# A two-layer decoder trunk: the first mixer's attention with its values stationary, two heads on the array's column halves, and probabilities scaled on GpSimd

## The reference, cut to what matters

```
# dilated: 4 slots; a slot joins three heads (window, dilation) = (128,1), (512,4), (2048,16)
s = q . k * scale, masked;  lse = logsumexp(s);  p = exp(s - lse);  out_g = p @ v
alpha = softmax over the three groups of lse;  o = sum_g alpha_g * out_g      # = one softmax over the three maps
# native sparse (NSA): 8 query heads, 2 key/value heads, three branches with a gate each
o = gate0 * softmax(q.k_cmp) @ v_cmp + gate1 * softmax(q.k_slc) @ v_slc + gate2 * softmax(q.k_win) @ v_win
out = concat(o_nsa, o_dil) @ w_out
```

## Time and profile before

| | before |
|---|---|
| median of 3 runs | 689.08 us (687.07 to 690.55) |
| the profiled execution: its time | 689.5 us |
| the profiled execution: its span | 687.5 us |
| PE busy | 668.7 us, 97% |
| DVE, ACT, POOL busy | 67%, 55%, 22% |
| chain that ended last | 92% PE |

### The profile page before, as it was taken

The page is one execution under the profiler, slowest core; times in us unless marked ns, Lnnn a source line. Parts: engine busy times, 40 slices in busy tenths (PEclk is TensorE's granted clock), DMA queues, the critical chain, the costliest instruction groups (busy, mean ns, idle before and its releaser), DMA issues.

```text
span 687.5 us, 10253 instructions
## 1 busy us (share of the span) xinstructions
PE 668.7 (97%) x3719; PEld 560.3 (82%) x3719; DVE 459.3 (67%) x620; ACT 380.4 (55%) x539; POOL 154.0 (22%) x117
## 2 busy tenths in 40 slices
PE   4999999999999999999999999999999999999996
PEld 3888887778788888888887999777788888888885
DVE  4596775577776878786547563576676878786532
ACT  5556435476476666767334634375475757676320
POOL 0021220000122434343001000372113343444000
PEclk9999999999999999999999999999999999999999
DMA  8957643001365353544752745301545353634601
GB/s 337 400 200 268 220 161 122 1 2 62 123 215 213 131 236 131 235 147 182 292 189 109 274 159 237 127 1 53 193 160 211 148 225 141 236 130 184 245 0 61
DMA packets 18651, 116.20 MB, mean 169 GB/s; under 512 B 2463, under 2 KB 3133, under 8 KB 5693
## 3 DMA queue, kind: packets, MB, share of 16 engines
q1 hardware_dynamic: 17325, 111.52, 43.3%
q10 hardware_dynamic: 1296, 4.26, 1.8%
HBM read 114.72 MB, written 1.05 MB: 168 GB/s over the span
## 4 chain that ended last, share of the span: by engine, by line
PE 92%; DVE 2%; ACT 2%; issue 2%; POOL 1%; DMA 1%; DVEq 0%; POOLq 0%
PE ps L1516 22%; PE ps L1155 13%; PE ps L1157 13%; PE ps L1156 13%; PE ps L1518 11%; PE ps L1197 5%; PE ps L1351 3%; PE ps L1277 1%; PE ps L1311 1%; PE ps L1150 1%; PE ps L1567 1%; PE ps L1437 1%; PE ps L1556 1%; PE ps L1287 1%; POOL rstd L1070 1%
## 5 line engine op out<-in xcount | busy, mean ns | idle before, releaser
L629 DVE TENSOR_TENSOR wlo<-raw,whi 128x2048 fp32r<-128x2048 f32 x99 | 226.0, 2311 | 69.6 <-ACT whi L333 69.5
L1516 PE MATMUL ps<-xpair,whi 128*128 128x512 f32 x640 | 226.4, 399 | 0.0
L333 ACT CAST whi<-raw 128x2048 fp32r<-128x2048 f32 x99 | 186.1, 1916 | 71.2 <-PE ps L1157 66.8
L1518 PE MATMUL ps<-xpair,wlo 128*128 128x256 f32 x640 | 179.8, 281 | 0.0
L1516 PEld LDWEIGHTS ps<-xpair,whi 128*128 128x128 f32 x640 | 120.3, 188 | 29.9
L1518 PEld LDWEIGHTS ps<-xpair,wlo 128*128 128x128 f32 x640 | 120.9, 189 | 0.0
L1110 POOL TENSOR_TENSOR hidf<-act_g,conv 128x512 f32<-128x512 f32 x22 | 74.6, 3392 | 83.9 <-ACT act_g L533 83.9
L1157 PE MATMUL ps<-whi,hid_lo 128*128 128x512 f32 x176 | 69.4, 395 | 0.0
L1156 PE MATMUL ps<-wlo,hid_hi 128*128 128x512 f32 x176 | 69.4, 394 | 0.0
L1155 PE MATMUL ps<-whi,hid_hi 128*128 128x512 f32 x176 | 69.4, 394 | 0.0
L1155 PE MATMUL ps<-whi,xpair 128*128 128x512 f32 x168 | 67.2, 400 | 0.2
(11 more groups left out here) (174 smaller groups left out, 987.5 us busy)
## 6 DMA issues: line engine op xcount, KB each, us to landing
raw<-in_weights SPq DMA_DIRECT2D x101, 1024.0 KB, 4.9
c_gpre<-in_gpre ACTq DMA_DIRECT2D x4, 512.0 KB, 4.7
raw<-in_weights SPq DMA_DIRECT2D x4, 512.0 KB, 8.5
c_gpost<-in_gpost ACTq DMA_DIRECT2D x4, 512.0 KB, 4.9
h<-in_x SPq DMA_DIRECT2D x2, 512.0 KB, 7.7
out<-h SPq DMA_DIRECT2D x4, 256.0 KB, 2.0
t<-in_masks SPq DMA_DIRECT2D x1, 512.0 KB, 14.1
c_rope<-in_rope SPq DMA_DIRECT2D x1, 256.0 KB, 14.0
```

The costliest lines, as they stand in the source:

```text
L333: act.copy(whi[:, slot, :], raw[:, slot, :]).then_inc(hi_done, 1)
L629: dve.tensor_tensor(wlo[:, slot, :], raw[:, slot, :], whi[:, slot, :].bitcast(F32), ALU.subtract).then_inc(lo_done, 1)
L1516: pe.matmul(ps[:, b0 + m, :], whi[:, slot, cols], xpair[:, kt].rearrange("p a c -> p (a c)"), start=kt == 0, stop=kt == KT - 1, skip_group ...
L1518: ins = pe.matmul(ps[:, b0 + m, 0:SEQ], wlo[:, slot, cols], xhi[:, kt, :], start=False, stop=kt == KT - 1, skip_group_check=True)
```

## The change

- **Values stationary.** `it_values` becomes `dil_values` and `nsa_values`. The 64 columns of values of a head are the stationary operand and 128 tokens of `probsT` move. The result comes out turned already, so `out_turn` and its copies' source change: `tile_hi` and `tile_lo` read the result bank.
- **Two heads on column halves.** The results of head e go to PSUM partitions 64e to 64e + 63, that is to one column half of the array, and the instructions of the two heads alternate.
- **Scaling.** A result whose tokens lie along the free axis can't be scaled per token, so the probabilities are: `it_coefs` on DVE (reciprocal, times gate) and then `it_scale` on GpSimd, in place in `probs`. `it_turn(n)` now waits for `it_scaled`. `it_output` and the separate results of the compressed branch go; that branch is one more matmul in `nsa_values`.
- **Order.** Dilated items come in pairs (slots 0 and 1, then 2 and 3), each pair with `t` = 1 first. `dil_qk` makes the scores of both with alternating rows, and waits for the exponentials of both items before. NSA items have `t` = 1 first too. `probs` and `probsT` have three buffers instead of two.

```diff
-        ITEMS = [("dil", j, t) for j in range(SLOTS) for t in range(TT)] + \
-                [("nsa", i, t) for i in range(NSA_PER) for t in range(TT)]
+        ITEMS = [("dil", 2 * pair + e, t) for pair in range(SLOTS // 2) for t in reversed(range(TT)) for e in range(2)] + \
+                [("nsa", i, t) for i in range(NSA_PER) for t in reversed(range(TT))]
...
@@ ACT
             for n in range(NI + 2):
                 if n < NI:
                     it_turned_out(n)
+                if n in TILE_OUT:
+                    tile_hi(TILE_OUT[n])
+                if n + 2 < NI:
+                    it_probs(n + 2)
                 if n == 0:
                     act.wait_ge(unit_used, EVEN_END["unit", 6])
                     act.copy(vbuf[:, :, 768:1280], ps[:, 6:8, :]).then_inc(in_free_act, 1)
-                if n - 2 in TURNS:
-                    it_hi(n - 2)
-                if n + 2 < NI:
-                    it_probs(n + 2)
...
@@ DVE
+            it_coefs(0)
+            it_coefs(1)
             compressed_probs()
             for n in range(NI + 2):
+                if n + 2 < NI:
+                    it_maxima(n + 2)
+                if 1 <= n and n + 1 < NI:
+                    it_coefs(n + 1)
                 if n < NI:
                     it_turned_out(n)
...
@@ POOL
+            def it_scale(n):
+                kind, _, t = ITEMS[n]
+                w, s, v = P * (t + 1), n % 3, n % 4
+                pool.wait_ge(it_coef, coefs_until(n))
+                if kind == "dil":
+                    pool.tensor_scalar(probs[:, s, 0:NG * w], probs[:, s, 0:NG * w], coef[:, v, 0:1], None,
+                                       ALU.mult).then_inc(it_scaled, 1)
+                    return
+                for m in range(4):
+                    ins = pool.tensor_scalar(probs[:, s, m * w:(m + 1) * w], probs[:, s, m * w:(m + 1) * w],
+                                             coef[:, v, 4 + m:5 + m], None, ALU.mult)
+                ins.then_inc(it_scaled, 1)
...
@@ PE
+            def dil_qk(n):
+                t = ITEMS[n][2]
+                w, tok = P * (t + 1), slice(t * P, (t + 1) * P)
                 if n >= 2:
-                    pe.wait_ge(it_exp, exps[n - 2])
+                    pe.wait_ge(it_exp, exps_until(n - 1))
+                for g in range(NG):
+                    for e in range(2):
+                        hd = g * SLOTS + ITEMS[n + e][1]
+                        rows = slice(HD * e, HD * e + HD)
+                        pe.matmul(psh[:, s_half(n + e) + g, 0:w], qkT[rows, TDQ + hd // 2, tok],
+                                  qkT[rows, TDK + hd // 2, 0:w], start=g != 1, stop=False, skip_group_check=True)
...
             def it_turn(n):
-                pe.wait_ge(it_exp, exps[n])
+                pe.wait_ge(it_scaled, n + 1)
...
+            def dil_values(n):
+                t = ITEMS[n][2]
+                o = tile_out(n, n + 1)
+                for m in range(NG):
                     for kt in range(t + 1):
                         k = m * (t + 1) + kt
-                        ins = pe.matmul(ps[:, bank, col:col + HD], probsT[:, s, k * P:(k + 1) * P],
-                                        vbuf[:, kt, v0:v0 + HD], start=k == 0, stop=k == maps * (t + 1) - 1,
-                                        skip_group_check=True)
+                        for e in range(2):
+                            v0 = V_DIL + (m * SLOTS + ITEMS[n + e][1]) * HD
+                            ins = pe.matmul(o[e * HD:(e + 1) * HD, :], vbuf[:, kt, v0:v0 + HD],
+                                            probsT[:, (n + e) % 3, k * P:(k + 1) * P], start=k == 0,
+                                            stop=k == NG * (t + 1) - 1, skip_group_check=True)
+                ins.then_inc(it_pv, 2)
...
+            it_turn(0)
+            dil_qk(2)
+            pe.wait_ge(in_free_act, EVEN_ACT)
+            it_turn(1)
+            for n in range(2, ND, 2):
+                if n + 2 < ND:
+                    dil_qk(n + 2)
+                else:
+                    nsa_qk(ND)
                 it_turn(n)
+                dil_values(n - 2)
+                if n + 2 == ND:
+                    nsa_qk(ND + 1)
+                it_turn(n + 1)
+                if n + 1 == PC_TURN:
+                    compressed_turn()
+            for n in range(ND, NI - 1):
+                if n + 2 < NI:
+                    nsa_qk(n + 2)
+                it_turn(n)
+                if n == ND:
+                    dil_values(ND - 2)
+                else:
+                    nsa_values(n - 1)
...
+            out_blocks("out0", 0, EVEN_KT, xhi, xlo, 0, 1, operand)
+            it_turn(NI - 1)
+            nsa_values(NI - 2)
+            out_blocks("out0", 0, EVEN_KT, xhi, xlo, 1, 3, operand)
+            nsa_values(NI - 1)
+            out_blocks("out0", 0, EVEN_KT, xhi, xlo, 3, 5, operand)
```

More of the change, by code:

```diff
@@ L282, in maps_of, with exps_until, coefs_until @@
             return NG if ITEMS[n][0] == "dil" else 4
+        def exps_until(n):
+            return sum(1 if kind == "dil" else 4 for kind, _, _ in ITEMS[:n + 1])
+        def coefs_until(n):
+            return sum(1 if kind == "dil" else 2 for kind, _, _ in ITEMS[:n + 1])
         block = ctx.enter_context(nc.Block())
@@ L870, in it_turned_out @@
                 dve.wait_ge(it_turned, n + 1)
[L871 to L878, removed]
+                if n >= 3:
+                    dve.wait_ge(it_pv, n - 2)
+                dve.tensor_copy(probsT[:, n % 3, BLK:k], ps[:, 5, 0:k - BLK]).then_inc(it_pT1, 1)
@@ L1095, in _ @@
                                        ALU.add).then_inc(staged, 1)
+            def it_scale(n):
[10 more added lines that the diff above has]
+                ins.then_inc(it_scaled, 1)
+            for n in range(NI):
+                it_scale(n)
             def junction(p):
@@ L1332, in it_values, with tile_out @@
-            def it_values(n):
-                kind, j, t = ITEMS[n]
-                s, bank = n % 2, 6 + n % 2
-                pe.wait_ge(it_pT0, n + 1)
-                if t:
-                    pe.wait_ge(it_pT1, wide_before(n) + 1)
-                if n >= 2:
-                    pe.wait_ge(it_o, outs[n - 2])
-                    if n - 2 in TURNS:
-                        pe.wait_ge(ot_lo, turns_before(n - 2) + 1)
-                maps = maps_of(n)
-                for m in range(maps):
-                    if kind == "dil":
-                        v0, col = V_DIL + (m * SLOTS + j) * HD, 0
-                    else:
-                        v0, col = (V_SLC, V_WIN)[m % 2] + (m // 2) * HD, m * HD
+            def tile_out(n, last):
+                tile, t = TILE_OF[n], ITEMS[n][2]
+                pe.wait_ge(it_pT0, last + 1)
+                if t:
+                    pe.wait_ge(it_pT1, wide_before(last + 1))
+                if t == TT - 1 and tile >= 2:
+                    pe.wait_ge(ot_lo, tile - 1)
+                return ps[:, 6 + tile % 2, t * P:(t + 1) * P]
@@ new lines, in dil_values, with nsa_values @@
+                ins.then_inc(it_pv, 2)
+            def nsa_values(n):
+                _, j, t = ITEMS[n]
+                o = tile_out(n, n)
+                pe.matmul(o, vc[:, 2 * j:2 * j + 2, :].rearrange("p m d -> p (m d)"), pcT[:, t, :], start=True, stop=False,
+                          skip_group_check=True)
+                for br in range(2):
+                    for kt in range(t + 1):
+                        for g in range(NSA_G):
+                            k, v0 = (2 * g + br) * (t + 1) + kt, (V_SLC, V_WIN)[br] + g * HD
+                            ins = pe.matmul(o[g * HD:(g + 1) * HD, :], vbuf[:, kt, v0:v0 + HD],
+                                            probsT[:, n % 3, k * P:(k + 1) * P], start=False,
+                                            stop=br == 1 and kt == t, skip_group_check=True)
+                ins.then_inc(it_pv, 1)
```

176 lines of the change are left out of this document (57 added, 119 removed).

## The result

The changed kernel takes 704.04 us (median of 4 runs, 703.19 to 704.91) beside 689.82 us of the kernel before on the same chip: a ratio of 1.0216 with a 95% interval of 1.0198 to 1.0233. The prediction of 683.2 us, faster, was wrong in sign, and the time lies outside its range. The profiled execution took 703.19 us.

What follows compares the result with a forecast made beforehand. PE was taken as the bound, busy 668.7 of 687.5 us. First output block 6.74 us earlier minus 0.8 back gives 5.9; 689.5 - 5.9 - 0.4 = 683.2 us, range 680.5 to 691.

Steps and rivals of the forecast that it cites:

- I take the casts, since the operation has one tensor input: Scaling on POOL priced like one-input casts: 0.83 us for 768 columns, 1.6 for four maps of a t = 1 NSA item.
- the two-input line: Rival on POOL's scaling: two-input price, 1.9 us for 768 columns, 2.9 for four maps; 690.2 us, no change; chance 0.15.
- The dearest rival: DVE holds POOL's scaling up: 2.2 us for 768 columns, 4.2 for four maps; 695.9 us, slower; chance 0.05.
- It decides for slower from some 3.6 us for the four maps on: Threshold in the rival of DVE holding POOL up: the kernel gets slower from some 3.6 us of scaling per four maps.
- The chain over two NSA items: NSA part: turn, copy, exponentials, coefficients, scaling and hand-overs take 5.6 us, so PE stays the bound by 0.2 us.
- the clock: TensorE's clock in the stage: read as full in the dilated and NSA parts; the sum had no term for it.
- the three waits of the dilated part: PE waits 2.3 us for the vbuf copy ahead of turn 1, then 1.3 each ahead of scores 4 and 6.
- the values of a dilated pair: Dilated part, values on PE: 1.48 us per pair with t = 1, 0.84 with t = 0.
- column halves run beside each other: Values on PE: two heads' instructions overlap; the rival that they don't gives 692 us, slower by 0.4%, chance 0.06.
- 5.8 us per NSA pair: NSA part: PE's own work for a pair of items takes 5.8 us against 6.45 before.
- 41.8 us from turn 0 to the first block: Turn 0 at 113.7 us, first block of the output projection at 155.5 instead of 162.24.
- the 0.8 given back in the projection: Output projection: turn 15, values 14 and values 15, 2.65 us, fall into it, giving 0.8 us back.

Runs made afterwards that it cites:

- e3: The changed kernel with unused bf16 matmuls filling PE's waits in the dilated part and ahead of turns 8, 10, 12 and 14: 697.32 us.
- e11: The changed kernel with GpSimd's scaling as one two-tensor multiplication per item, coefficients broadcast along the columns: 689.99 us.
- e2: The changed kernel with the same scalings on VectorE, directly behind the item's coefficients, instead of on GpSimd: 688.49 us.
- e6: e2 with unused bf16 matmuls (11, 10, 10) in PE's three waits of the dilated part: 685.81 us.
- e4: The changed kernel with the scaling left out, each turn waiting for the coefficients alone: 685.63 us.
- e8: e2 with the vbuf copy ahead of item 2's exponentials, dilated values ahead of the next scores, and output projection blocks 3 and 4 as before the change: 686.64 us.
- e9: e2 with the vbuf copy ahead of item 2's exponentials, compressed probabilities behind item 2's maxima, and projection blocks 3 and 4 as before the change: 682.73 us.
- e12: e11 with e9's orders and projection tail, and exponentials 3 and 5 ahead of the copies of turns 1 and 3 on ScalarE: 683.0 us.

## Why the prediction was wrong

**The step that failed** is "I take the casts, since the operation has one tensor input". A float32 `tensor_scalar` on GpSimd does not run at the price of a cast: 2.26 us for 768 columns against 0.83, 3.69 for four maps against 1.6. The rows of before had a second reading, the two-input line, which I gave 0.15, and even that was too low (1.9 and 2.9). The dearest rival named nearly the right size, 2.2 and 4.2 us, and got 695.9 us out of it, but by luck, for a cause that is hardly there: VectorE holding POOL up. The scalings of the NSA items last the same whatever VectorE does beside them (shortest, median and longest, ns, 16 of 128 columns and 16 of 256):

```profile
L1088 POOL TENSOR_SCALAR probs<-probs,coef x32: 602/763/923, 140.5 to 171.2; 128x256 f32<-128x256 f32 x16, 128x128 f32<-128x128 f32 x16
```

Only the second scaling of 768 columns lasted longer, 2.41 us against 2.20 to 2.21 of the other three, and the runs don't show why. VectorE's work for the compressed branch, which does not read PSUM as the prediction had it of all such work, ran beside it and beside the first one, which took 2.21. e3, which has the dear price and a full clock, took 697.3, within 1.5 of that rival's sum. "It decides for slower from some 3.6 us for the four maps on" was right too, and the four maps took 3.69.

**The mechanism was right where the size was not.** The chain over two NSA items was 5.6 us with 1.6 of scaling in it; with 3.69 it is 7.7, and the turns stand 7.7 apart. With the scaling on VectorE (1.4 for four) they stand 5.3 to 6.0 apart, by PE's own work, and with e11's 1.89, 6.0, where the chain would have 5.9.

**What the sum had no term for** is the clock. I took it as 1.00 because the earlier trace rows showed that, though the forecast itself had PE wait 2.3, 1.3 and 1.3 us within 10.5 us (115.6 to 126.05). It cost 6.7 us in the changed kernel (e3) and 2.7 in e2 (e6). It fell in e4 too. With e6's 2.7 taken off, which is an estimate, since e4 wasn't run with the filler, e4 would be at 682.9, beside the 683.2 that I had forecast with a cheap scaling. Nor did the sum have the 0.7 us of the moved block (e8).

**Where the 19.6 us between forecast and profiled execution are** (683.6 against 703.2): turn 0 1.4 late (115.14 against 113.7), by the wait of 1.45 for the first scaling, 14.9 between turn 0 and the first block (56.7 against 41.8), 1.9 up to the junction (21.6 against 18.9 + 0.8: the 0.7 of the tail, and 1.1 more, of the clock that was still at 0.62 there, since e3 has 20.5), and a rest of 1.4, nearly all behind the junction, where kernels that differ in nothing there scatter by 3.7.

**What held:** the three waits of the dilated part (forecast 2.3, 1.3 and 1.3; measured 2.09, 1.25 and 1.24, with the releasers named); the values of a dilated pair (1.48; measured 1.47, from 126.73 to 128.20), so that column halves run beside each other also when instructions alternate within one bank; 5.8 us per NSA pair once the scaling is cheap (e2); 41.8 us from turn 0 to the first block (42.1 in e6, which is the kernel that meets the forecast's terms, with a cheap scaling, a full clock and the old orders; the 42.2 of e4 and the 41.8 of e9 are luck, since there a lower clock makes up for work or waits that are missing); the 0.8 given back in the projection (e9 has 19.8 to the junction against 18.9). The orders on VectorE and ScalarE, which I only priced as waits, could have been read as repairs: e9 and e12 take some 6 and 7 us out of e2 and e11 by them (the 0.7 of the tail included), and without them the change gains next to nothing (e2 1.1 us below the kernel before, e11 none).

**The Trainium skill** (GPSIMD Engine Reference, "Elementwise — side-by-side cycle accounting") spoke against this change, and its direction was right. It has GpSimd at 2.6 cycles an element where VectorE needs one, and puts the 2.6 down to an operation with two inputs. Here the slope is 2.64 ns a column for `tensor_scalar` (2256 - 1244 over 384) and 0.52 on VectorE (621 - 420 over 384), five to one, and 1.67 ns for GpSimd's multiplication of two tensors with a broadcast, three to one against the same 0.52. The measurement decides: the form with fewer tensor inputs is the dearer one, and by more than the page's ratio.

**Open:** why a column costs more in the one-tensor form than in the two-tensor form on GpSimd, and why 512 columns of two tensors cost 1302 ns in the earlier trace rows and 1041 with the broadcast in e11. Neither was taken apart. That the clock fell because PE stood idle is shown by e3 and e6. The runs go no further than that.

## What to carry to other kernels

Where an operation has no row in the trace, the nearest row is not its price but one end of a range, and an operation that goes onto the chain that releases the bound engine should be costed at the dear end, or measured alone first: here the same multiplication cost 3.69, 1.89 or 1.4 us for four maps, by engine and form. Any forecast that adds waits to a busy TensorE should carry a term for the clock: the 5.1 us of waits in the dilated part cost 2.7 more in e2, and useless matmuls in the waits bought it back. When a wait is taken away, look for what ends second: the wait of 2.6 ahead of turn 1 became 1.4 and then 0.9, under another engine's name.

## What the hardware did that I had not expected

- GpSimd's `tensor_scalar` in float32: 602 ns for 128 columns, 922 for 256, 2256 for 768 (2.20 us undisturbed); with a constant 528, 847 and 2131. The two-tensor multiplication with a broadcast coefficient: 827 ns for 384 columns and 1894 for 1024.
- TensorE at the lower clock behind waits of 2.09 and 1.25 us, of 2.79, and of 3.18: eight transposes 1.97 us for 1.09. The granted clock was 0.50 from 146 to 150 us and 0.94 from 150 to 154.
